# The first input unit in two halves of its features, the first half ahead of two modulation pieces

## The reference

```python
c_act = silu(c)
mod = c_act @ w_ada[l] + b_ada[l]                 # 1024 x 6144
shift1, scale1, gate1, shift2, scale2, gate2 = split(mod, 6)
hdn = rmsnorm(x, norm1_g[l]) * (1.0 + scale1) + shift1
proj = hdn @ w_in[l]                              # 1024 x 7200, cut in units of 464 and 512 columns
```

## Time and profile before

| | |
|---|---|
| median of 3 runs | 1745.09 us (1743.43 to 1746.32) |
| profiled execution | 1743.61 us |
| its span | 1741.9 us, 24848 instructions |
| PE busy | 1684.2 us (97%) |
| DVE busy | 1180.3 us (68%) |
| ACT busy | 857.8 us (49%) |
| loads and stores | 323.71 MB, mean 186 GB/s |

### The profile page before, as it was taken

One profiled execution on the slowest core, in us unless ns is written; L12 is line 12 of the kernel. 1 busy time (PEld: TensorE's weight loads), 2 busy tenths in 40 slices (PEclk: granted clock), 3 DMA queues, 4 the chain that ended last, 5 costly groups with the idle time before them and its releaser, 6 DMA issues.

```text
span 1741.9 us, 24848 instructions
## 1 busy us (share of the span) xinstructions
PE 1684.2 (97%) x9315; PEld 1389.8 (80%) x9315; DVE 1180.3 (68%) x2033; ACT 857.8 (49%) x1505; POOL 147.1 (8%) x296
## 2 busy tenths in 40 slices
PE   6999999999999999999999999999999999999998
PEld 3887785689878886774899878767998787679986
DVE  5776565866776975547735676666788767667885
ACT  3354463455443442661555354575554544755542
POOL 1210101000000000210000010041000100410000
PEclk8999999999999999999999999899999999999999
DMA  9887335557855974337465646604665566046552
GB/s 344 294 283 263 122 97 167 191 195 249 297 156 192 347 252 164 121 98 231 147 213 186 194 144 224 175 1 156 196 187 185 162 214 185 1 144 207 182 184 83
DMA packets 185912, 323.71 MB, mean 186 GB/s; under 512 B 13540, under 2 KB 101184, under 8 KB 185792
## 3 DMA queue, kind: packets, MB, share of 16 engines
q1 hardware_dynamic: 183200, 320.54, 56.5%
q10 hardware_dynamic: 2592, 1.57, 0.3%
HBM read 321.02 MB, written 1.05 MB: 185 GB/s over the span
## 4 chain that ended last, share of the span: by engine, by line
PE 71%; DVE 15%; ACT 5%; DMA 3%; issue 3%; POOL 2%; SPq 0%; DVEq 0%; POOLq 0%; ACTq 0%
PE bank L741 67%; DVE ring_r L1813 6%; PE bank L750 3%; ACT sm L1458 2%; DMA ring<-in_w_in 1%; DMA ring<-in_w_ada 1%; POOL sm L667 1%; DVE ada L1918 1%; ACT high L1372 1%; DVE gates_r L1838 1%; DVE sm L1998 1%; DMA ring<-in_w_ff 1%; DVE oT L1882 0%; DVE gates L2496 0%; DVE oT_r L1845 0%
## 5 line engine op out<-in xcount | busy, mean ns | idle before, releaser
L1813 DVE TENSOR_TENSOR ring_r<-ring,high 128x1024 fp32r<-128x1024 f32 (+3 forms) x390 | 460.5, 1197 | 266.1 <-ACT high L1372 258.1
L1372 ACT ACTIVATE high<-ring 128x1024 fp32r<-128x1024 f32 (+3 forms) x390 | 402.0, 1037 | 480.2 <-PE bank L741 353.4
L741 PE MATMUL bank<-ring_r,featT_r 128*128 128x512 f32 (+3 forms) x928 | 354.9, 382 | 0.0
L741 PE MATMUL bank<-high,featT_r 128*128 128x512 f32 (+3 forms) x712 | 276.5, 388 | 8.3 <-DVE oT_r L1845 2.6
L741 PE MATMUL bank<-featT_r,high 128*128 128x256 f32 x960 | 272.9, 284 | 0.0
L741 PE MATMUL bank<-featT_r,ring_r 128*128 128x256 f32 x960 | 271.6, 283 | 0.0
L741 PE MATMUL bank<-oT_r,high 128*128 128x256 f32 x960 | 271.6, 283 | 0.0
L741 PE MATMUL bank<-high,oT_r 128*128 128x512 f32 (+3 forms) x712 | 270.1, 379 | 0.0
L741 PE MATMUL bank<-high,gates_r 128*128 128x512 f32 x736 | 230.2, 391 | 3.6 <-DVE ring_r L1813 2.6
L741 PEld LDWEIGHTS bank<-ring_r,featT_r 128*128 128x128 f32 x928 | 175.5, 189 | 27.0 <-issue 0.5
L741 PEld LDWEIGHTS bank<-oT_r,high 128*128 128x128 f32 x960 | 184.2, 192 | 0.6 <-issue 0.5
(11 more groups left out here) (267 smaller groups left out, 2204.7 us busy)
## 6 DMA issues: line engine op xcount, KB each, us to landing
ring<-in_w_ff SPq DMA_DIRECT2D x128, 512.0 KB, 4.6
ring<-in_w_ada SPq DMA_DIRECT2D x96, 512.0 KB, 5.8
ring<-in_w_up SPq DMA_DIRECT2D x176, 256.0 KB, 3.5
ring<-in_w_in SPq DMA_DIRECT2D x64, 464.0 KB, 5.3
ring<-in_w_in SPq DMA_DIRECT2D x48, 512.0 KB, 5.2
ring<-in_w_in SPq DMA_DIRECT2D x48, 474.0 KB, 4.8
ring<-in_w_down SPq DMA_DIRECT2D x44, 512.0 KB, 3.4
ring<-in_w_out SPq DMA_DIRECT2D x24, 512.0 KB, 4.7
```

The costliest lines, as they stand in the source:

```text
L741: ins = pe.matmul(o, a, b, start=start, stop=stop, skip_group_check=True)
L1372: act.activation(it["high"], it["raw"], ACT.Copy).then_inc(high_ready, 1)
L1813: dve.tensor_tensor(it["low"], it["raw"], it["high"].bitcast(F32), ALU.subtract).then_inc(low_ready, 1)
```

## The change

In the stream, the first two pieces of unit 0 go between PE's and DVE's w_ada pieces of half 0 and those of half 1; its last two stay behind all w_ada pieces. PE multiplies both token tiles with the first two pieces (features 0 to 511) behind the first two of its four w_ada pieces of half 1, and the other half of unit 0 at the end. The banks of unit 0 are one of `for_act` (tile 0) and one of `for_dve` (tile 1) in place of `outputs` and `for_dve`. ACT makes the first two high parts ahead of the features of half 0 and the other two behind them, copies the second row, makes the second half's features of tile 1 (new `last_features` on ACT), and then issues the small loads. DVE makes the first two low parts and the low features of half 0 ahead of its four steps of half 1, the second half's features of tile 0, and the low features of tile 1 (`last_lows`). ACT now copies tile 0 of unit 0 out, as it does for all units behind it.

```diff
             if l == 0:
-                for it in pe_ada:
+                begun = [cols_piece(w_in[l], k0, k0 + 2, (0, ATT_W), split=True) for k0 in range(0, KD, 2)]
+                for n, it in enumerate(pe_ada):
+                    if n == 4:
+                        for j in range(2):
+                            put(begun[j], spare_1[j], True, 12)
+                    if n == 6:
+                        for j in range(2):
+                            used(begun[j])
                     put(it)
                     ada_piece()
+                for j in range(2, 4):
+                    put(begun[j], spare_1[j], False, 12)
+                split_units.append(begun)
+                low_units.append(begun)
             layer1_at.append(len(stream))
             for u in range(11):
+                if u == 0 and l == 0:
+                    continue
...
-            def tokens_as_ready(second=None):
+            def tokens_in_halves():
                 get, n = next_quarters()
+                rings = for_act, for_dve
+                open_ = [claim(r)[0] for r in rings]
+                def half_of(i):
+                    for t in range(T):
+                        for j in (2 * i, 2 * i + 1):
+                            w = get(j)
+                            for kk in range(2):
+                                c = 2 * j + kk
+                                features(c, [t])
+                                three(open_[t][:, 0:n], feature_parts(c, slice(t * P, t * P + P)), (w[0][:, kk, :], w[1][:, kk, :]),
+                                      c == 0, c == KD - 1, rings[t].full if c == KD - 1 else None)
+                            if t:
+                                owed.append((piece_used, 1))
+                return half_of
...
-                    if j == 0 and between is not None:
+                    if j == n and between is not None:
                         between()
...
                     modulation_pair(0, lambda: [flip_tile(scaled, t) for t in range(T)])
-                    modulation_pair(1)
-                    tokens_as_ready()
+                    halves = []
+                    def first_half():
+                        halves.append(tokens_in_halves())
+                        halves[0](0)
+                    modulation_pair(1, first_half)
+                    halves[0](1)
...
+            def last_features(gain, shift):
+                act.wait_ge(for_dve.full, 2)
+                for f in range(4, 8):
+                    ins = act.activation(featF[:, f, P:2 * P], for_dve.banks[1][:, (f - 4) * P:(f - 3) * P], ACT.Identity,
+                                         scale=gain[:, f:f + 1], bias=shift[:, f:f + 1])
+                link(ins)
+                act.wait_ge(for_dve.read, 1)
+                act.sem_inc(for_dve.read, 1)
+                act.activation(featT_r[:, 4:8, P:2 * P], featF[:, 4:8, P:2 * P], ACT.Copy).then_inc(feat_high, 1)
...
                 if l == 0:
                     gain_out(0)
+                    highs(2)
                     seen.more(evac_dve)
                     features_out(gain, shift, True)
+                    highs(2)
                     gain_out(1)
-                    highs(4)
                     seen.more(evac_dve)
+                    last_features(gain, shift)
                     late_rows()
...
                     for half_ in range(2):
+                        if half_:
+                            first_quarters(2)
+                            for t in range(T):
+                                first_lows(t)
                         for j in range(4):
                             ada_step()
...
                         if half_:
-                            for t in range(T):
-                                first_lows(t)
-                            first_quarters(1)
+                            first_quarters(2)
                         both_out(half_)
                         dve.sem_inc(evac_dve, 1)
-                    last_features(gain, shift, 0)
-                    first_quarters(1)
-                    last_features(gain, shift, 1)
-                    first_quarters(2)
+                    last_features(gain, shift)
+                    last_lows()
```

More of the change, by code:

```diff
@@ L1563, in _ @@
                     highs(4)
-                    if u < (2 if l else 1):
-                        if l == 0:
-                            late_small()
+                    if u < 2 and l:
                         continue
+                    if u == 0:
+                        late_small()
                     b = tile()
@@ L1855, in first_lows, with last_lows, last_features @@
                                   ALU.subtract).then_inc(feat_first, 1)
-            def last_features(gain, shift, t):
-                cols = slice(t * P, (t + 1) * P)
+            def last_lows():
+                got[id(for_dve)] += 1
+                seen.more(feat_high)
+                dve.tensor_tensor(featL[:, 4:8, P:2 * P], featF[:, 4:8, P:2 * P], featT_r[:, 4:8, P:2 * P].bitcast(F32),
+                                  ALU.subtract).then_inc(feat_last, 1)
+            def last_features(gain, shift):
+                cols = slice(0, P)
                 b = tile(for_dve)
@@ L2157, in _ @@
                     n = min(ATT_W, ATT - c0)
-                    if u == 0:
-                        b = tile(outputs)
-                        read(outputs, dve.tensor_copy(proj[:, 0, c0:c0 + n], b[:, 0:n]))
                     b = tile(for_dve)
```

## The result

The changed kernel takes 1747.52 us in the median of 20 runs (1744.18 to 1750.77), the kernel before 1744.74 (1740.87 to 1747.9, also 20). The ratio of the two is 1.0019, 95% interval 1.0013 to 1.0025: 3.3 us slower (2.3 to 4.4; the medians themselves differ by 2.8), at the edge of what was called no change, 0.2%. The forecast was 1745.8, the range 1742.8 to 1749.0.

The account below looks back on a forecast made before the run. Bandwidth, then a latency chain, then PE were taken to bound the opening. Unit 1's start, 0.65 us later, added to 1743.61 gave 1744.3; 1.5 more for the median gave 1745.8 us, range 1742.8 to 1749.0.

Parts of the forecast that it names:

- What bounds the opening: First 50 us: bandwidth to about 31 us, a latency chain to 41, then PE; later work moves with unit 1.
- The first half: Unit 0's first 24 products on PE, at 0.21 us each, were to run from 26.45 to 31.5 us.
- The ring wait: Loads of w_in pieces 2 and 3 wait for slots: issued 30.65 and 32.45, landing 3.4 us later.
- Bias addition at 38.95: DVE adds the bias at 38.95 us, 33.00 before, behind the late pieces, row copy and small products.
- The second half: Unit 0's last 24 products on PE: from 42.2 us, 8.5 at half clock, ending at 48.8, at latest 51.5.
- B: The time of DVE's bias addition: between 37.2 and 39.0 us, taken as 38.95.
- ACT's queue is late next: ACT's 18 small loads, 7.1 us of issue, delay unit 1's high parts; its first product comes at B+11.6, 50.55 us.
- The sum: Unit 1 starts at the later of 48.8 and 50.55 us: 0.65 later, within -1.1 to +1.6.
- (a): Opening: PE's gain is swallowed by ACT's issue queue, total 1744.0 to 1746.7 us; chance 0.78.
- (d): Opening: PE's clock falls in the first half, unit 1 starts 6.7 us later, total 1751.8 us; chance 0.05.
- (c): Opening: w_in pieces 2 and 3 land late, at 8.8 us total 1751.2 us; chance 0.10.
- Unit 0's copy on ACT, broadcasts four pieces later: Behind the opening: a 0.6 us copy moves from DVE to ACT and gate-row broadcasts come later, at no cost.

Follow-up runs that it names:

- the change kept busy: The change with 11 extra PE products on constants, 4 in the wait for the row copy and 7 ahead of the second half; ratio 1.0011 to the kernel before.
- row first: The change with ACT copying the gain row between the third and fourth high parts and issuing small loads behind the first half's features; 0.9987 of the kernel before.
- the kernel before kept busy: The kernel before with 12 extra PE products on constants in three idle stretches; ratio 0.9971, on the repeat 0.9979, to the kernel before.
- the halved one: The change with two low parts written elsewhere and small loads behind the first half's features; 0.9993 of the kernel before, 0.9973 with seven extra products.

## Why the prediction was right or wrong, point by point

**What bounds the opening**: right. The start of unit 1 moved by 2.7 us; from there to unit 3 and on to 500 us a shift of 2.7 to 3.2 us persists, and the median moved by as much. Later stretches took back 2 us of it in the one profiled execution (2.6 us under the median of its kernel).

**The first half**: right in place, 0.5 to 0.7 us late. It was to run from 26.45 to 31.5 at 0.21 us a product; it ran from 26.99 to 32.18. The row products ahead were partly at half clock (0.54 granted in 21.9 to 25.3), which the profile of the kernel before did not show. It is not the change's: seven of the twelve later profiles were free of it (granted 1.00 in that stretch), the one of the change kept busy among them, which runs the same work up to there as the change, and the second one of the kernel before kept busy, which runs the work of the kernel before up to 29 us, has it (0.61). So it varies between executions. The two profiles of the same work without it issue piece 2 at 30.55 and 30.50 for 31.24 here, and copy the row at 37.58 and 37.54 for 37.89, so 0.3 us of the 2.7 at unit 1 are this execution's chance.

**The ring wait**: right in mechanism, 0.7 to 1.2 us too small. The issues came at 31.24 and 33.2 (said: 30.65 and 32.45), from issue to use it was 3.5 and 3.8 us where 3.4, the shortest from issue to landing, was taken. (The fit that the prediction set beside it, of the Trainium skill, "DMA: Bandwidth & Descriptors", is given there for DMAs that GpSimd issues; these are SP's, and its 3.1 us was 0.4 and 0.7 too short here.) The sum had the price; what it missed is that the price was avoidable, since only the row copy's place behind it cost anything (row first).

**Bias addition at 38.95**: it was 40.51. Of the 1.56 us, 1.0 is the late landing and the late half, and 0.8 that the small products with the gain row ran at half clock (1.85 us for 1.05), less 0.25 of hand-over that had been counted. The clock was priced in the second half alone, and had already fallen ahead of it, at about 38.7.

**The second half**: ready at B+3.4 (said 3.25), 12.3 of 24 products at half clock where 8.5 were taken; it ended at 51.3, inside the 48.8 to 51.5 given.

**ACT's queue is late next**: right, and shown (the change kept busy). The loads started at B+2.31 (said 2.3), unit 1 at B+12.08 (said 11.6); the 0.34 us between the last issue and the first high part had been taken as 0.04.

**The sum**: +0.65 forecast with bounds of -1.1 and +1.6; the opening gives +2.7 and the ratio of the runs +3.3. The forecast mechanism (a) is the one that happened, but not its size: the median, 1747.5, lies above the 1744.0 to 1746.7 given to it with a chance of 0.78. Its upper bound was too tight, because it bounded one cost at a time and the clock touched three of them (the row products ahead of the first half, the small products, the second half). The term that failed most is the bias addition. Rival (d), a clock that falls in the first half, happened in a mild form (0.5 us), and (c), late landings, by 0.4 us. The whole range held since it had room for a part of (c) and for a slow start of unit 1. The slow small products, 0.8 us, were in neither, so that it held is in part luck.

**Unit 0's copy on ACT, broadcasts four pieces later**: nothing of it shows; the gap at unit 3 kept its 1.00 us.

The Trainium skill ("TensorE: Matmul & The Clock Gate", "The HAM clock gate") says that PE's clock is throttled by default and that activity releases it. The runs agree for the second half: it took 7.4 us without extra products and 5.1 with them. The stretch in 21.9 to 25.3 us, in which PE was busy without a gap and granted 0.54, is not explained by it here.

## What to carry to other kernels

Before work is moved ahead in a latency chain, ask what is queued behind the chain's end on every engine, DMA issues too: 18 small loads on ACT had 6.7 us of slack, the change moved them by 8.9, and 3.5 us won on PE later turned into a wait (the change kept busy). An engine's copy that others wait for had better not stand behind an operand whose load waits for a slot. And where PE idles in front of a dense stretch, price the clock; a few products in the gap were worth more here (3.7 to 5.1 us in the kernel before, of which 1 us was located; 3.5 in the halved one) than the reordering (at best 2.3 without them), and at most 1.4 us, inside the intervals, where ACT's queue was the last wait (1.0019 to 1.0011).

## What was not expected of the hardware

The granted clock was also low while PE was running one-column products without a gap (0.54 granted, 3.40 of 3.40 us busy, in 21.9 to 25.3 us of the changed kernel), and in the same place stayed at full in other executions (eight of the fourteen profiles were granted 1.00 there, the others 0.54 to 0.67). Elsewhere the same instructions were granted half clock for stretches whose share differed (0.77 or 0.83 over 30 us near 1130), so a difference of 1 to 3 us between two single profiles of this kernel says nothing until its place is found.
